# GpSimd issues the cached value pages, and the prompt scores are computed from high and low halves

## The reference

```python
h = rmsnorm(x, g_mix_pre)
q, k, v, xr, gb, gates = split(h @ w_in)
k_all = concat([k_past, k]); v_all = concat([v_past, v])   # pages of the cache, through page_table
logits = einsum('bhqd,bhqjkd->bhqjk', q, kg) * HEAD_DIM ** -0.5 + bias   # 8 heads of 64
p = softmax(where(mask, logits, NEG_INF))
o_attn = einsum('bhqjk,bhqjkd->bhqd', p, vg)
# beside it: conv of 4 taps, RG-LRU scan, gelu(gb); then the merge by gates, w_out, rmsnorm, SwiGLU FFN
```

## Time and profile before

| | |
|---|---|
| median of three runs | 780.96 us |
| the profiled execution | 781.89 us |
| its span, first to last instruction | 779.8 us |
| granted TensorE clock, mean | 0.997 |
| PE busy | 766.1 us (98%) |
| DVE (VectorE) busy | 482.4 us (62%) |
| ACT (ScalarE) busy | 357.2 us (46%) |
| POOL (GpSimd) busy | 70.4 us (9%) |

### The profile page before, as it was taken

How to read it: one execution, slowest core, us unless ns; L and a number is a source line. 1 busy time by engine, 2 the same in 40 slices (tenths; PEclk the granted TensorE clock), 3 DMA queues, 4 the chain that set the end, 5 groups by cost and what they waited for, 6 DMA issues and landing times.

```text
span 779.8 us, 16411 instructions
## 1 busy us (share of the span) xinstructions
PE 766.1 (98%) x5975; PEld 724.2 (93%) x5975; DVE 482.4 (62%) x756; ACT 357.2 (46%) x625; POOL 70.4 (9%) x156
## 2 busy tenths in 40 slices
PE   8999999999999999999999999999999999999996
PEld 6879999999899899997799999999999999999996
DVE  4655756847647634774567987887777777222323
ACT  5436534534625532334456555455555565222322
POOL 5521102102012010004000000000000010000000
PEclk9999999999999999999999999999999999999998
DMA  6745655555544224516552333233333125434333
GB/s 191 180 110 114 161 127 111 151 131 123 142 110 111 65 85 142 183 55 182 169 163 55 109 108 99 83 87 108 108 108 107 55 76 169 117 94 107 90 92 126
DMA packets 196979, 91.68 MB, mean 118 GB/s; under 512 B 65142, under 2 KB 190538, under 8 KB 196940
## 3 DMA queue, kind: packets, MB, share of 16 engines
q1 hardware_dynamic: 194270, 84.63, 40.0%
q0 software_dynamic: 2576, 6.45, 2.7%
q10 hardware_dynamic: 94, 0.09, 0.1%
HBM read 82.37 MB, written 6.81 MB: 114 GB/s over the span
## 4 chain that ended last, share of the span: by engine, by line
PE 94%; POOL 2%; DMA 1%; ACT 1%; issue 0%; DVE 0%; DVEq 0%; POOLq 0%; ACTq 0%
PE ps L958 32%; PE ps L1312 27%; PE ps L1377 17%; PE ps L1211 6%; PE ps L1281 3%; PE ps L1070 1%; PE ps L1084 1%; PE ps L1102 1%; PE ps L987 1%; DMA bias_rev<-dist_shift 1%; PE ps L1144 1%; PE ps L1055 1%; PE ps L1219 1%; PE ps L1115 1%; PE ps L990 0%
## 5 line engine op out<-in xcount | busy, mean ns | idle before, releaser
L1923 DVE TENSOR_TENSOR w_lo<-w_raw,w_hi 128x1024 fp32r<-128x1024 f32 (+1 forms) x67 | 80.1, 1197 | 131.7 <-ACT w_hi L1450 131.4
L958 PE MATMUL ps<-xin_hi,w_hi 128*128 128x272 f32 x576 | 125.4, 297 | 2.1 <-DVE w_lo L1923 1.0
L1450 ACT ACTIVATE w_hi<-w_raw 128x1024 fp32r<-128x1024 f32 (+1 forms) x68 | 70.0, 1030 | 119.3 <-PE ps L1377 78.1
L958 PE MATMUL ps<-xin_hi,w_lo 128*128 128x272 f32 x576 | 120.4, 288 | 0.0
L958 PE MATMUL ps<-xin_lo,w_hi 128*128 128x272 f32 x576 | 120.2, 288 | 0.0
L958 PEld LDWEIGHTS ps<-xin_hi,w_hi 128*128 128x128 f32 x576 | 90.4, 189 | 10.9 <-issue 7.6
L958 PEld LDWEIGHTS ps<-xin_lo,w_hi 128*128 128x128 f32 x576 | 91.1, 189 | 0.0
L958 PEld LDWEIGHTS ps<-xin_hi,w_lo 128*128 128x128 f32 x576 | 90.6, 189 | 0.0
L1377 PE MATMUL ps<-hid_hi,w_hi 128*128 128x272 f32 (+2 forms) x352 | 75.4, 289 | 0.4 <-DVE hid_lo L2339 0.4
L1377 PE MATMUL ps<-hid_lo,w_hi 128*128 128x272 f32 (+2 forms) x352 | 74.9, 288 | 0.0
L1377 PE MATMUL ps<-hid_hi,w_lo 128*128 128x272 f32 (+2 forms) x352 | 74.9, 288 | 0.0
(11 more groups left out here) (337 smaller groups left out, 1748.8 us busy)
## 6 DMA issues: line engine op xcount, KB each, us to landing
w_raw<-in_w_in_dram SPq DMA_DIRECT2D x72, 256.0 KB, 3.5
g_raw<-in_w_gate_up_dram SPq DMA_DIRECT2D x40, 256.0 KB, 3.7
w_raw<-in_w_down_dram SPq DMA_DIRECT2D x40, 256.0 KB, 3.0
u_raw<-in_w_gate_up_dram SPq DMA_DIRECT2D x20, 256.0 KB, 3.1
e_raw<-in_w_gate_up_dram SPq DMA_DIRECT2D x20, 256.0 KB, 4.2
kc<-in_cache_k_dram SPq DMA_DIRECT2D x64, 64.0 KB
vc<-in_cache_v_dram SPq DMA_DIRECT2D x64, 64.0 KB
wo_raw<-in_w_out_dram SPq DMA_DIRECT2D x12, 256.0 KB, 4.1
```

What stands on the lines that cost most here:

```text
L958: mm = e.matmul(ps[:, bank + h, 0:HT], wt[:, kw, :], xt[:, kx, h * HT:h * HT + HT], start=first and wt is wh and xt is xh, stop=last and ( ...
L1450: e.activation((to or w_hi[s])[:, 0:k, :], w_raw[s][:, 0:k, :], ACT.Copy).then_inc(hi_done, count)
L1923: e.tensor_tensor(wl[:, 0:k, :], w_raw[s][:, 0:k, :], wh[:, 0:k, :].bitcast(F32), ALU.subtract).then_inc(lo_done, count)
```

## The change

Four things are done. GpSimd issues the value pages of all pairs, reads the page numbers itself (six while it waits for its first DMAs, ten after the issue of `bias_rev`), and its loop over pairs is written out as a first pair, a loop and a last pair. In pair 0 the order on GpSimd becomes: spread of the queries, own masks, the four copies (`ready`), 16 value pages; in the others the pages of the next pair follow the gelu cubic. SyncE loses its value pages; keys of pair 0 are split in 6 and 10 around the weights of tile 2, and the keys of pair 1 are loaded as those of the other pairs. The prompt scores become three passes over rounded halves: ScalarE writes `q_hi` and `k_hi`, VectorE writes `q_lo` and `k_lo`, 512 columns each, and TensorE waits for both low halves ahead of `scores(3)`. Two semaphores of the FFN weights are merged into one.

```diff
-KC_PAGES_0 = (), (), (), (), (), range(0, 4), range(4, 9), range(9, 14)
...
-                    if j in (2, 4) and first:
-                        load_values(0, range(4 * j - 8, 4 * j))
-                    if j < 4 and not first:
-                        if j == 0:
-                            load_keys(it, KC_REST)
-                            e.wait_ge(mi_ready, it * 5 - 3)
-                        load_values(it, range(4 * j, 4 * j + 4))
...
-            load_keys_0()
+            load_keys_0(range(6))
             load(2, 0, wi[:, :, 2 * 512:2 * 512 + P])
+            load_keys_0(range(6, DEC_B * NPG))
             load(3, 1, wi[:, :, 3 * 512:3 * 512 + P])
...
+            page = page_numbers(range(6))
             e.wait_ge(bias_moved, 16 * DEC_T + 16)
             for f in range(PAIRS):
                 e.dma_start(bias_rev[:, f, :], ...
+            page += page_numbers(range(6, DEC_B * NPG))
...
+            def load_values(it):
+                for j in range(DEC_B * NPG):
+                    src = cache_v[0].rearrange("n t h d -> n t (h d)")[bass.ds(page[j], 1), :, bass.ds(it * P, P)]
+                    e.dma_start(vc[:, j, :], src.rearrange("o (i a) c -> a (o i) c", i=BLK)).then_inc(vc_in, 16)
...
+            def pair(it, first=False, last=False):
+                if first:
+                    e.wait_ge(consts, C_ZERO + PAIRS + DEC_B)
+                    spread(it)
+                    e.wait_ge(q_spread, 1)
+                    own_mask()
+                    ready(it)
+                    load_values(it)
+                else:
+                    ready(it)
+                    e.wait_ge(it_ready, it + 1)
+                    spread(it)
...
+                if not last:
+                    e.wait_ge(mi_ready, it * 5 + 2)
+                    load_values(it + 1)
...
+                    if qts[0] == Q_ORDER[0]:
+                        e.wait_ge(qk_lo, it * 2 + 2)
                     for qt in qts:
-                        for h in range(2):
-                            rows = slice(DH * h, DH * h + DH)
-                            mm = e.matmul(ps[:, SCORE_BANK[h], score_cols(qt)], qT[rows, qt * P:(qt + 1) * P],
-                                          kT[rows, 0:(qt + 1) * P], start=True, stop=True)
+                        for q, k in ((q_hi, k_hi), (q_lo, k_hi), (q_hi, k_lo)):
+                            for h in range(2):
+                                rows = slice(DH * h, DH * h + DH)
+                                mm = e.matmul(ps[:, SCORE_BANK[h], score_cols(qt)], q[rows, qt * P:(qt + 1) * P],
+                                              k[rows, 0:(qt + 1) * P], start=q is q_hi and k is k_hi, stop=k is k_lo)
...
+                e.activation(q_hi[:, :], qT[:, 0:SEQ], ACT.Copy).then_inc(qk_hi, 1)
...
+                e.activation(k_hi[:, :], kT[:, 0:SEQ], ACT.Copy).then_inc(qk_hi, 1)
...
+                def q_low():
+                    e.wait_ge(qk_hi, it * 2 + 1)
+                    e.tensor_tensor(q_lo[:, :], qT[:, 0:SEQ], q_hi[:, :].bitcast(F32), ALU.subtract).then_inc(qk_lo, 1)
+                def k_low():
+                    e.wait_ge(qk_hi, it * 2 + 2)
+                    e.tensor_tensor(k_lo[:, :], kT[:, 0:SEQ], k_hi[:, :].bitcast(F32), ALU.subtract).then_inc(qk_lo, 1)
...
-                e.wait_ge(u1_in[s], uses * 16 + 16)
-                e.wait_ge(u2_in[s], uses * 16 + 16)
+                e.wait_ge(u_in[s], uses * 32 + 32)
```

More of the change, by code:

```diff
@@ L197, in program @@
     st_out = put("st_out", [36, DR], where=[lgt_at])
-    bd_all = put("bd_all", [P, 2, PAIRS, RGB], where=[gates_at + 4 * PAIRS * GT_IT * T])
+    w = [gates_at + 4 * PAIRS * GT_IT * T]
+    bd_all = put("bd_all", [P, 2, PAIRS, RGB], where=w)
+    q_hi, k_hi, k_lo = (put(n, [P, SEQ], F32R, where=w) for n in ("q_hi", "k_hi", "k_lo"))
+    assert w[0] <= stage_at
+    q_lo = put("q_lo", [P, SEQ], F32R, where=[stage_at])
     prT = put("prT", [P, 2, PT_W, P], where=[kcT_at])
@@ L374, in program @@
         q_spread = sem("q_spread")
+        qk_hi = sem("qk_hi")
+        qk_lo = sem("qk_lo")
         s_ready = sem("s_ready")
@@ L606, in load_keys, with load_keys_0 @@
                                 ).then_inc(kc_in, 16)
-            def load_keys_0():
-                for j in range(DEC_B * NPG):
+            def load_keys_0(pages):
+                for j in pages:
                     e.dma_start(kc[:, j, :], page_of(cache_k, 0, j).rearrange("o t c -> t (o c)")).then_inc(kc_in, 16)
[L613 to L617, removed]
             def store_blocks(out, buf, it):
@@ L836, in _, with page_numbers @@
             e.dma_start(dist_bias, drow[:, :]).then_inc(bias_moved, 16)
+            e.wait_ge(page_in, 16)
+            def page_numbers(js):
+                return [e.value_load(pages[0:1, j:j + 1], min_val=0, max_val=n_phys - 1) for j in js]
+            page = page_numbers(range(6))
             e.wait_ge(bias_moved, 16 * DEC_T + 16)
@@ L847, in _, with own_mask, ready @@
                               ).then_inc(consts, 1)
[L848 to L857, removed]
+            def own_mask():
+                for f in range(PAIRS):
+                    own = bias_s[:, f, PAST:KS].rearrange("p (j g t) -> p j g t", j=NJ, g=NG)
+                    e.wait_ge(consts, C_ZERO + PAIRS + DEC_B + 2 * f)
+                    e.affine_select(out=own, in_=own, compare_op=ALU.is_ge, fill=NEG,
+                                    base=0, pattern=[[-8, NJ], [-GR, NG], [0, DEC_T]], channel_multiplier=1).then_inc(consts, 1)
+                    e.wait_ge(consts, C_ZERO + PAIRS + 1 + DEC_B + 2 * f)
+                    e.affine_select(out=own, in_=own, compare_op=ALU.is_ge, fill=NEG,
+                                    base=7, pattern=[[8, NJ], [GR, NG], [0, DEC_T]], channel_multiplier=-1).then_inc(consts, 1)
+            def load_values(it):
+                for j in range(DEC_B * NPG):
+                    src = cache_v[0].rearrange("n t h d -> n t (h d)")[bass.ds(page[j], 1), :, bass.ds(it * P, P)]
+                    e.dma_start(vc[:, j, :], src.rearrange("o (i a) c -> a (o i) c", i=BLK)).then_inc(vc_in, 16)
+            def ready(it):
                 count = e.to_reg(it + 1)
@@ L868, in _, with spread @@
                               ).then_inc(it_ready, 1)
+            def spread(it):
                 count = e.to_reg(it * 4 + 2)
@@ L872, in _ @@
                 e.wait_ge(tile_free[0], count)
-                e.wait_ge(it_ready, it + 1)
                 for h in range(2):
@@ L906, in _ @@
                               ).then_inc(st_saved, 1)
+            pair(0, first=True)
+            with e.Fori(1, PAIRS - 1) as it:
+                pair(it)
+            pair(PAIRS - 1, last=True)
             e.wait_ge(rg_done, PAIRS + 1)
@@ L2057, in heads @@
                     k_copy(); cache_copy(3)
+                    q_low()
                     next_lo(2)
@@ L2063, in heads @@
                     keys_turn(2); keys_turn(3)
+                    q_low()
                     k_copy()
                     next_lo(2)
+                k_low()
                 count, ready = e.to_reg(it * 5 + 1), e.to_reg(it + 1)
```

21 lines of the change are left out of this document (12 added, 9 removed).

## The result

The changed kernel took 785.84 us, the median of 22 runs (781.48 to 788.18); the kernel before took 779.38 us, in 22 runs on the same chip. The ratio is 1.0072, 95% interval 1.0058 to 1.0086: slower by 0.7%. That is +5.6 us, where -2.1 was forecast (778.8 us, with a range of 777.2 to 783.2). The changed kernel's runs lie in two groups, nine at 781.5 to 783.1 and thirteen at 785.1 to 788.2; the profiled execution, 782.62 us with a span of 780.6, is of the lower one.

A forecast was written before the change was run, and what follows sets the result against it. TensorE was taken as the bound, 94% of the chain of waits. The terms -1.74 + 0.4 - 0.8 sum to -2.1 us, giving 778.8 us from the 780.96 median, range 777.2 to 783.2.

The forecast's parts named there:

- The values of the other pairs: GpSimd's value pages after the gelu cubic: 10 to 14 us fit in 18.41 us idle, wanted 50 us later; hidden.
- TensorE waits for nothing of SyncE's in the pairs: 0: SyncE loses 64 issues; since TensorE waits for none of its work in the pairs, the term is 0.
- Slower by over 0.3%: Outcome above 783.3 us, chance 0.14: 0.09 for heads one after the other, plus the far end of late values.
- matmuls that don't pair: Rival: in the prompt scores TensorE takes the two heads' passes in turn, 6.8 us more, 786.4; chance 0.09.
- late values: Rival: pair 0's values land late and `values_s` waits 1.5 to 5.2 us, around 781.4; chance 0.22.
- The spread comes earlier: Pair 0: the spread ahead of the masks ends at 39.0, before TensorE's need at 42.54, removing the `q_bd` wait; -1.74 us.
- what is late next: Pair 0 check after the spread: samples' softmax scaling ends at 46.5, wanted at 47.3; cover 0.8 us, nothing lost.
- The keys of pair 0: Their pages still come before they are turned at 31.89; 0 us, with 1.7 at stake for the slowest landing.
- The values of pair 0: GpSimd issues them from 44.8 at 0.64 us a page, in at 58.1, wanted at 58.05; +0.4 us.
- The rival by the rule on the shared port: VectorE's fp32 scalings block GpSimd's DMA descriptors, pushing the last pages back some 1.3 us; 780.1, one way into late values.
- as they are in the sequence: VectorE's holds of GpSimd, such as the 1.19 us copy to `prm_it`, were left unchanged in pair 0's timing.
- The scores: Prompt scores in three rounded passes, two heads side by side, save 0.20 us a pair; -0.8 us for four, ends -1.3 and +6.8.

The follow-up runs named there:

- f2: Changed kernel with the value pages of pairs 1 to 3 issued by SyncE as before, only pair 0's by GpSimd; 779.73 us, ratio 1.0007 to the kernel before.
- f1: Spread first and three passes, pair 0's values on SyncE, pairs 1 to 3's on GpSimd, keys as before the change; 787.11 us, ratio 1.0097.
- e5: Kernel before with only GpSimd's order in pair 0 changed, the spread before the masks; 779.41 us, ratio 0.9999.
- m: Changed kernel with GpSimd issuing only pair 0's value pages, SyncE the others, keys ordered and timed as before; 778.04 us, ratio 0.998 to the kernel before.
- e4: Changed kernel with all cached values back on SyncE and both key schedules as before; 778.36 us, ratio 0.9992 to the kernel before.
- e1: Kernel before with only the prompt scores in three passes, their four copies and the merged semaphore; 778.78 us, ratio 1.0004.

## Why the prediction was wrong

**The step that failed** is "The values of the other pairs": "16 x 0.64 to 0.85 = 10 to 14 us fits, and they are wanted 50 us later. Hidden." The issues did fit (10.08 us for 15) and the values were in time. But the cost was asked only of GpSimd, which issues, and of TensorE, which waits for the values; not of what shares the DMA engines. Put at nothing, this term measured 5.1 us (f2 against the changed kernel). The sentence next to it, "TensorE waits for nothing of SyncE's in the pairs: 0", took a small slack for a large one: TensorE stood for no weights of SyncE's, but ScalarE did (2.18 us at 81.33), and the lead at the end of pair 0 was 4.2 us in one profile and 2.7 in the other. In f1, 7.8 us of delay in SyncE's queue became 4.3 of waiting. None of my rivals had it. "Slower by over 0.3%" had 0.14: 0.09 on matmuls that don't pair, the rest on late values.

The Trainium skill (DMA: Bandwidth & Descriptors, "Issuing engines are not separate DMA queues") says that transfers started by ScalarE, SyncE or GpSimd run on the same 16 DMA engines and interleave. The runs agree, with 13.84 us against 6.07 for the same five pages. This rule spoke against the change, and I had weighed another.

**The spread comes earlier, -1.74.** The mechanism was right: it ended at 36.0, earlier than the 39.0 I gave, and no wait for `q_bd` is left. The size was that of one late start; in the second profile the wait was 0.7, and the reordering alone (e5) gained nothing in the median. And the gain was to be kept by the line "what is late next", which I followed through the samples' softmax only. Next were the keys (1.0, 0.7 and 0.7 us in three profiles of the change) and SyncE's weights (`probs_T`, 1.0, 1.3 and 2.7).

**The keys of pair 0, "0, with 1.7 at stake":** about 1 us of the stake was lost; TensorE reached them at about 30 instead of 31.89. With the `probs_T` wait the new order of the keys costs 2.1 us (f2 against m); the prediction asked only for the keys' own landing.

**The values of pair 0, +0.4 us:** close; it was 0. 0.67 us a page against 0.64; 16 issues from 40.17 instead of 44.8: 2.1 of that is the earlier start-up, 1.0 the copy to `prm_it`, which took 0.18 us and not 1.19. That is luck: no wait at `values_s` in three profiles, and one of 2.4 and of 0.5 in the two kernels where such a copy was held. The tile `vc` after the change (durations in ns, least, median, most; the landing answers the earlier trace rows):

```profile
L865 POOL DMA_DIRECT2D vc<-in_cache_v_dram x64: 677/677/719, 40.2 to 210.3; - x64
...
DMA to landing us min/median/max: 2.7/3.9/7.2
```

The rival by the rule on the shared port didn't show in the issues: VectorE's fp32 scalings at 44.20 (0.37 us), 47.96 (0.53) and 48.67 (0.49) lie inside the burst, and no issue of the 64 took over 0.719 us. What did push the burst back, in two other kernels, is the hold of GpSimd's copies, which the prediction left "as they are in the sequence".

**The scores, -0.8 us:** right in sign and somewhat small: -0.28 a pair where 0.20 was forecast, so -1.1 for four; the three pairs behind pair 0 show it as 675.5 to 674.7. The three pieces took 0.91, 0.73 and 0.84 us against 0.92, 0.74 and 0.90 forecast, 2.48 in place of 2.76 a pair; the two heads run side by side. (The lower end of that term, -1.3, was reckoned with 0.41 ns a column for "the old steps", which by the prediction's own working took 0.82.) In the medians it can't be told: e4 (0.9992) against e5 (0.9999) has the sign, and e1 (1.0004) has not.

**The sum.** From the first weights to pair 1's `scores_s`: -1.7 for `q_bd`, +1.0 keys, +1.0 `probs_T`, +2.9 more for `w_lo` (3.9 against 1.0) and -0.3 for the scores of pair 0 is +2.9 of the +3.8 measured; some 0.9 us has no row of its own. The clock adds to it in the runs where it falls. In the medians, by the ratios: pair 0's values on GpSimd with the spread and the passes (m) -1.6 us, the order of the keys +2.1, the values of pairs 1 to 3 +5.1, together +5.6; each interval is 1 us or more to either side.

## What to carry to other kernels

Moving DMAs to an idle engine frees issue time, not DMA engines: before moving them, look at what the old queue carries in the same microseconds, how small its pieces are, and how far ahead of its use what stands behind them is. The lead is read before the change, from where the weights are ready to where their tile begins, and an engine that is not the bound but already stands for them is its sign. A burst costs where the other queue's lead is shortest, so place it where the lead is long. And a start-up that varies by 2.8 us makes one profile's waits poor prices: take a second profile before a wait of 1.7 us is called the bound.

## What the runs showed of the hardware

A key page of 64 KB in 512 pieces of 128 bytes occupies SyncE's queue for 1.1 to 1.7 us, the mean of groups of four and five, and for 2.4 to 3.1 us (9.49 for four, 13.84 for five, 12.43 for four) while GpSimd issues value pages. That isn't so for the first ones always: the first four beside pair 0's burst in the changed kernel took 6.42, and the half weight tile behind them 2.80. In 128 pieces of 512 bytes a key page takes 0.48 to 0.65 us alone and 0.48 to 0.75 beside the burst. Half a weight tile (256 KB) took 4.89 us to issue at 75.07, where behind the start-up it took 0.4 to 1.8 in the kernel before.

Copies of GpSimd of 8 and 24 columns took 1.19 and 1.21 us beside VectorE's `w_lo`, and 0.18 and 0.20 us otherwise.

GpSimd's own issues keep to 0.68 us in the median whatever SyncE does, but its queue pauses by count. After the change the third and fourth bursts were

```profile
132.63 10.74 POOL L865 DMA_DIRECT2D vc<-in_cache_v_dram  x16
...
193.75 9.42 POOL L865 DMA_DIRECT2D vc<-in_cache_v_dram  x14
...
209.62 1.37 POOL L865 DMA_DIRECT2D vc<-in_cache_v_dram  x2 [6.45 <-issue]
```

so pauses of 6 us stand behind page 31 (16 + 15) and page 62 (31 + 1 + 16 + 14). Eight other profiles with GpSimd's bursts pause behind the 31st page as well, by 4.8 to 6.2 us. Nothing waited for it here. The cause was not looked for.
